# A transformer block in fp32 on one core: weight sums of the down projection paced one to a step, and SBUF tiles moved by 32 bytes

## What is computed

```python
h    = rms_norm(x, pre_mix_norm)
proj = h @ w_in
A    = forgetting_attention(fq, fk, fv, log_f)       # 8 heads x 64, causal, per-key decay
B    = gated_delta_chunked(q, k, v, g, beta)         # 4 heads x 128, chunks of 64, behind a short conv
x    = x + rms_norm(concat(A, B) @ w_out, post_mix_norm)
h    = rms_norm(x, pre_mlp_norm)
y    = square(relu(h @ w_up)) @ w_down
x    = x + rms_norm(y, post_mlp_norm)
```

## Time and profile before

| | us |
|---|---|
| median of 3 runs | 1527.16 (1526.25 to 1529.45) |
| the profiled execution, its own time | 1522.94 |
| its span | 1521.2 |
| PE busy in the span | 1408.3 (93%) |
| DVE busy | 998.5 (66%) |
| POOL busy | 679.5 (45%) |
| ACT busy | 650.0 (43%) |

### The profile page before, as it was taken

The page is one execution under the profiler, slowest core; times in us unless marked ns, Lnnn a source line. Parts: engine busy times, 40 slices in busy tenths (PEclk is TensorE's granted clock), DMA queues, the critical chain, the costliest instruction groups (busy, mean ns, idle before and its releaser), DMA issues.

```text
span 1521.2 us, 20643 instructions
## 1 busy us (share of the span) xinstructions
PE 1408.3 (93%) x7389; PEld 1179.0 (78%) x7389; DVE 998.5 (66%) x1506; ACT 650.0 (43%) x1342; POOL 679.5 (45%) x582
## 2 busy tenths in 40 slices
PE   6899999968989899898799989999999998999997
PEld 5688888857878889797688767888878776788885
DVE  6767777746566665765535697666676589744557
ACT  6554334435454553554423442233233343445453
POOL 3633333217365482753500366666567169440001
PEclk9999999989999999999799989999999999999999
DMA  6133333254132031012222224444444983333533
GB/s 202 42 119 107 108 111 111 84 181 138 29 98 70 29 98 43 15 43 65 82 90 84 76 84 152 153 153 152 153 152 139 339 309 132 95 97 95 208 97 143
DMA packets 135324, 177.87 MB, mean 117 GB/s; under 512 B 10492, under 2 KB 82732, under 8 KB 135224
## 3 DMA queue, kind: packets, MB, share of 16 engines
q1 hardware_dynamic: 135224, 176.56, 36.3%
HBM read 124.05 MB, written 52.48 MB: 116 GB/s over the span
## 4 chain that ended last, share of the span: by engine, by line
PE 60%; DVE 15%; POOL 11%; issue 5%; DMA 5%; ACT 2%; SPq 1%; POOLq 0%; DVEq 0%; ACTq 0%
PE ps L2625 6%; PE ps L2566 6%; PE ps L2568 6%; PE ps L2567 6%; PE ps L2884 5%; PE ps L2885 5%; PE ps L2886 5%; DMA w_bot<-in_w_up_dram 4%; DVE db_lo L2179 3%; DVE da_lo L2177 3%; PE ps L2750 3%; PE ps L2871 2%; PE ps L2872 2%; PE ps L2873 2%; PE ps L2825 2%
## 5 line engine op out<-in xcount | busy, mean ns | idle before, releaser
L2884 PE MATMUL ps<-db_hi,da_hi 128*128 128x512 f32 x448 | 177.6, 396 | 10.7 <-DVE db_lo L2179 10.7
L2886 PE MATMUL ps<-db_hi,da_lo 128*128 128x512 f32 x448 | 174.6, 390 | 0.0
L2885 PE MATMUL ps<-db_lo,da_hi 128*128 128x512 f32 x448 | 174.5, 389 | 0.0
L2177 DVE TENSOR_TENSOR da_lo<-a_raw,da_hi 128x512 fp32r<-128x512 f32 x112 | 103.4, 923 | 100.3 <-ACT da_hi L1663 100.3
L1663 ACT ACTIVATE da_hi<-a_raw 128x512 fp32r<-128x512 f32 x112 | 70.7, 631 | 172.4 <-PE ps L2886 150.0
L2871 PE MATMUL ps<-bt_hi,ring_hi 128*128 128x512 f32 x320 | 127.4, 398 | 3.9 <-DVE ring_lo L2099 3.6
L2873 PE MATMUL ps<-bt_hi,ring_lo 128*128 128x512 f32 x320 | 128.1, 400 | 0.0
L2872 PE MATMUL ps<-bt_lo,ring_hi 128*128 128x512 f32 x320 | 127.8, 399 | 0.0
L2436 POOL TENSOR_TENSOR o_rs<-o_ms,halves 128x1 f32<-128x1 f32 x24 | 16.5, 689 | 226.9 <-DVE o_ms L2202 111.4
L2566 PE MATMUL ps<-i_bt_hi,i_ring_hi 128*128 128x512 f32 x280 | 111.5, 398 | 3.2 <-DVE i_u L1852 3.2
L2884 PEld LDWEIGHTS ps<-db_hi,da_hi 128*128 128x128 f32 x448 | 84.0, 188 | 38.7 <-DVE db_lo L2179 21.9
(11 more groups left out here) (351 smaller groups left out, 3754.2 us busy)
## 6 DMA issues: line engine op xcount, KB each, us to landing
a_raw<-act_dram SPq DMA_DIRECT2D x112, 256.0 KB, 2.7
act_dram<-s_act SPq DMA_DIRECT2D x64, 256.0 KB, 2.0
wd<-in_w_down_dram SPq DMA_DIRECT2D x15, 1024.0 KB, 6.8
act_dram<-c SPq DMA_DIRECT2D x48, 256.0 KB, 4.9
w_top<-in_w_up_dram SPq DMA_DIRECT2D x18, 512.0 KB, 4.6
w_bot<-in_w_up_dram SPq DMA_DIRECT2D x16, 512.0 KB, 5.8
i_top<-in_w_in_dram SPq DMA_DIRECT2D x14, 512.0 KB, 4.0
i_bot<-in_w_in_dram SPq DMA_DIRECT2D x14, 512.0 KB, 5.3
```

Of the source, the lines that this page charges most:

```text
L2177: nc.vector.tensor_tensor(da_lo[s][:, :], a_raw[n % 4][:, :], da_hi[s][:, :].bitcast(F32), ALU.subtract).then_inc(d_lo_ready, 1)
L2884: nc.tensor.matmul(acc, da_hi[s][:, cols], db_hi[s][:, :], start=start, stop=False, skip_group_check=True)
L2885: nc.tensor.matmul(acc, da_hi[s][:, cols], db_lo[s][:, :], start=False, stop=False, skip_group_check=True)
L2886: return nc.tensor.matmul(acc, da_lo[s][:, cols], db_hi[s][:, :], start=False, stop=stop, skip_group_check=True)
```

## The change

Two things change. Both are in the table of addresses and in GpSimd's part of the projection down.

Addresses: every tile that started 32 bytes past a multiple of 64 now starts 32 bytes lower, on a multiple of 64 (147424 becomes 147392, 163808 becomes 163776, and so on). To make room `sums` moves from 147392 to 146944, inside a tile of constants that is used only earlier. The new addresses are 64 bytes past a multiple of 128, all of them.

```diff
-        gate_w_hi = placed("gate_w_hi", 204768, [P, KT, P], F32R)
-        gate_w_lo = placed("gate_w_lo", 208864, [P, KT, P], F32R)
+        gate_w_hi = placed("gate_w_hi", 204736, [P, KT, P], F32R)
+        gate_w_lo = placed("gate_w_lo", 208832, [P, KT, P], F32R)
...
-        I_BT_AT = {6: 147424, 7: 163808, 5: 180192, 4: 196576, 3: 212960}
+        I_BT_AT = {6: 147392, 7: 163776, 5: 180160, 4: 196544, 3: 212928}
...
-        sums = placed("sums", 147392, [P, 2, 4])
+        sums = placed("sums", 146944, [P, 2, 4])
...
-        big_hi = placed("big_hi", 163808, [P, KT, SEQ], F32R)
-        big_lo = placed("big_lo", 196576, [P, KT, SEQ], F32R)
+        big_hi = placed("big_hi", 163776, [P, KT, SEQ], F32R)
+        big_lo = placed("big_lo", 196544, [P, KT, SEQ], F32R)
...
-        BT_AT = {6: 147424, 7: 163808, 5: 180192, 4: 196576, 3: 212960}
+        BT_AT = {6: 147392, 7: 163776, 5: 180160, 4: 196544, 3: 212928}
...
-        wd = {(0, 0): placed("wd11", 45184, [P, FP, HALF]), (1, 0): placed("wd21", 147424, [P, FP, HALF]),
-              (1, 1): placed("wd22", 180192, [P, FP, HALF]), (0, 1): placed("wd12", 77952, [P, FP, HALF])}
+        wd = {(0, 0): placed("wd11", 45184, [P, FP, HALF]), (1, 0): placed("wd21", 147392, [P, FP, HALF]),
+              (1, 1): placed("wd22", 180160, [P, FP, HALF]), (0, 1): placed("wd12", 77952, [P, FP, HALF])}
```

```diff
+        PACE = {7: (8, 2), 6: (9, 2), 4: (8 + 2 * FP, 1), 5: (9 + 3 * FP, 1)}
+
         def t_count(i, kf):
-            return 3 * FP + kf + 1 if i == 5 else 3 * kf + {7: 1, 6: 2, 4: 3}[i]
+            return 2 * kf + {7: 1, 6: 2}[i] if i in (7, 6) else {4: 2, 5: 3}[i] * FP + kf + 1
...
             def t_part(i, kf):
                 b11, b12, b21, b22 = (wd[q][:, kf, :] for q in ((0, 0), (0, 1), (1, 0), (1, 1)))
+                if i in PACE:
+                    pool.wait_ge(d_lo_ready, 2 * (PACE[i][0] + PACE[i][1] * kf))
...
             for kf in range(FP):
-                for i in (7, 6, 4):
+                for i in (7, 6):
                     t_part(i, kf)
             for kf in range(FP):
+                t_part(4, kf)
+            for kf in range(FP):
                 t_part(5, kf)
```

More of the change, by code:

```diff
@@ L385, in build @@
         conv_rows = placed("conv_rows", 146880, [TAPS * 3 * GDN_HEADS, P])
-        x_in = [placed(f"x_in{s}", at, [P, D]) for s, at in enumerate((212960, 217056, 221152, 225248, 196576, 200672))]
+        x_in = [placed(f"x_in{s}", at, [P, D]) for s, at in enumerate((212928, 217024, 221120, 225216, 196544, 200640))]
         x_n = [placed(f"x_n{s}", 127232 + 4096 * s, [P, D]) for s in range(2)]
@@ L391, in build @@
         pre_row = placed("pre_row", 139520, [P, D])
-        gate_w = placed("gate_w", 163808, [P, KT, P])
-        gate_w_hi = placed("gate_w_hi", 204768, [P, KT, P], F32R)
-        gate_w_lo = placed("gate_w_lo", 208864, [P, KT, P], F32R)
+        gate_w = placed("gate_w", 163776, [P, KT, P])
+        gate_w_hi = placed("gate_w_hi", 204736, [P, KT, P], F32R)
+        gate_w_lo = placed("gate_w_lo", 208832, [P, KT, P], F32R)
         gate_y = placed("gate_y", 131328, [P, SEQ])
@@ L435, in build @@
         z_tok = [placed(f"z_tok{s}", at + 20480, [P, NT, P]) for s, at in enumerate(SET_AT)]
-        mixed_half = [placed(f"mixed_half{s}", at, [P, HT, D]) for s, at in enumerate((94336, 147424))]
+        mixed_half = [placed(f"mixed_half{s}", at, [P, HT, D]) for s, at in enumerate((94336, 147392))]
         k_split = [placed(f"k_split{s}", 110720 + 4096 * s, [P, SEQ], F32R) for s in range(2)]
@@ L459, in build @@
         wait_holder = placed("wait_holder", 146272, [P, 1])
-        c_raw = {"z": placed("c_raw_z", 163808, [P, SEQ]), "v": placed("c_raw_v", 167904, [P, SEQ]),
-                 "k": placed("c_raw_k", 180192, [P, SEQ]), "q": placed("c_raw_q", 184288, [P, SEQ])}
+        c_raw = {"z": placed("c_raw_z", 163776, [P, SEQ]), "v": placed("c_raw_v", 167872, [P, SEQ]),
+                 "k": placed("c_raw_k", 180160, [P, SEQ]), "q": placed("c_raw_q", 184256, [P, SEQ])}
         c_first = {"z": c_raw["z"], "v": c_raw["v"], "k": placed("c_first_k", 20608, [P, SEQ]), "q": placed("c_first_q", 73856, [P, SEQ])}
         v_fox_first = placed("v_fox_first", 28800, [P, SEQ])
[L465 to L478, removed]
+        v_fox = placed("v_fox", 171968, [P, SEQ])
+        decay = placed("decay", 176064, [P, NT, P])
+        kn = placed("kn", 188352, [P, 4, P])
+        qn = placed("qn", 190400, [P, 4, P])
+        knT = placed("knT", 192448, [P, 4, P])
+        qnT = placed("qnT", 194496, [P, 4, P])
+        kbg = placed("kbg", 196544, [P, 2, 4, P])
+        vb = placed("vb", 200640, [P, 2, 4, P])
+        kbT = placed("kbT", 204736, [P, 4, P])
+        n_low = placed("n_low", 208832, [P, 2, 4, P])
+        n_lev = placed("n_lev", 212928, [P, 2, 4, P])
+        t_inv = placed("t_inv", 217024, [P, 2, 4, P])
+        r_inv = placed("r_inv", 221120, [P, 2, 4, P])
+        xb = placed("xb", 225216, [P, 2, 4, P])
         gate_ps = banks(6, 2)
@@ L718, in build @@
         db_lo = [placed(f"db_lo{s}", at + 6144, [P, HALF], F32R) for s, at in enumerate(D_AT)]
-        wd = {(0, 0): placed("wd11", 45184, [P, FP, HALF]), (1, 0): placed("wd21", 147424, [P, FP, HALF]),
-              (1, 1): placed("wd22", 180192, [P, FP, HALF]), (0, 1): placed("wd12", 77952, [P, FP, HALF])}
+        wd = {(0, 0): placed("wd11", 45184, [P, FP, HALF]), (1, 0): placed("wd21", 147392, [P, FP, HALF]),
+              (1, 1): placed("wd22", 180160, [P, FP, HALF]), (0, 1): placed("wd12", 77952, [P, FP, HALF])}
         c_bot = placed("c_bot", 110720, [P, HT, D])
-        c_top = placed("c_top", 212960, [P, HT, D])
+        c_top = placed("c_top", 212928, [P, HT, D])
         sq_buf = placed("sq_buf", 135296, [P, D])
```

## The result

The changed kernel takes 1511.71 us (median of 4 runs, 1508.85 to 1514.60), the kernel before beside it 1527.66 (1526.25 to 1529.45): a ratio of 0.9901, 95% interval 0.9886 to 0.9916. It is 16 us faster; 28.5 had been forecast, and the time lies above the range of 1492 to 1510. The profiled execution took 1514.45 us with a span of 1512.7.

The account below looks back on a forecast made before the run. TensorE's matmul pace was taken to bound most projection stretches, VectorE's collisions with GpSimd the stretch from 1246 to 1310.9 us. From 1527.2 us, 12.5 (pacing) and 16.0 (addresses) were subtracted: 1498.7 us, range 1492 to 1510.

Parts of the forecast that it names:

- What bounds the kernel: TensorE's matmul time in most projection stretches; from 1246 to 1310.9 us VectorE, slowed by GpSimd, 1.09 us per collision.
- Part 1: Projection down: weight sums paced at most one per step return 19 slow steps from 3.40 to 2.72 us; 12.5 us won.
- The backlog: Projection down, steps 12 to 15: sums released late cause about seven collisions; 0.5 us of stall, between 0 and 1.5.
- Part 2: Projections in, out, up and gates: all operands on multiples of 64 bring matmuls to 0.2267 us; 16.5, less 0.5: 16.0 us.
- The addresses give nothing, as 128 counts: Rival, chance 0.10: operands still differ against 128 bytes, so the new addresses win nothing; 1514.7 us.
- TensorE's gain turns into waits: Rival, chance 0.06: stages end on another engine's work, so half of the addresses' gain is lost; 1506.7 us.
- Against: the room of VectorE and GpSimd: Argument against the rival of waits: in the projection up VectorE is busy 118.73 of 175 us, GpSimd 108.45.
- The other two rivals: Pacing gains nothing as collisions go on (0.02, 1511.2 us); an offset of 64 bytes costs more than 32 (0.02, 1529.3 us).
- the remark on the clock: Attention starts earlier and its clock's falls may shift; if a tenth of up to 25 us shifts, 2.5 us either way.

Follow-up runs that it names:

- e1: The kernel before with the paced weight sums alone, every tile at its old address: 1517.21 us, ratio 0.9926.
- e4: The changed kernel run again, unchanged: 1512.92 us, ratio 0.9913 to the kernel before.
- e3: A separate kernel without the layer: TensorE alone, 36 matmuls for each of 16 pairs of tile offsets; 0.2267 to 0.2339 us per matmul.
- e2: The kernel before with the new addresses alone, the sums in their old order: 1525.48 us, ratio 0.9980.
- e5: The changed kernel with its upper tiles another 64 bytes lower, at 128 modulo 256: 1506.17 us, ratio 0.9870 to the kernel before.
- e6: As e5, with rings 6 and 7 of the projection in also moved, 128 bytes higher: 1507.51 us, ratio 0.9875 to the kernel before.

## Why the prediction was wrong

**What bounds the kernel** was right: pace where TensorE fills the stretch, collisions from 1246 to 1311 us.

**Part 1 was right.** Forecast 12.5 us, between 11.5 and 13; e1 alone wins 12.2 at one clock and 12.8 in the projection down's own length. The steps are 2.72 us, the sums 1.29, the waits those foretold. The backlog cost 0.4 us (steps 14 and 15 took 3.00 and 2.85) where 0.5 was taken, and 0.2 to 0.8 in the profiles of e1 and e4. So a collision's 1.09 us from the rows came nearer than the Trainium skill's full exclusion (SBUF — State Buffer, Who interferes with whom), by which it would have been 2.0. The Trainium skill calls all contention of the two engines there an exclusive lock; "fully blocks" stands with VectorE's two-port modes, and an instruction with two SBUF inputs is said to contend. Not foreseen were 1.1 us at steps 6, 7 and 8 (3.04, 3.37 and 2.88 us), where `a_raw` lands late. They are no price of the change: the second profile of before has 1.0 us there too, and e1 has none.

**Part 2 was mis-sized, and this is where the prediction failed.** The step is "a matmul is slow where its two operands lie differently against 64 bytes. After the change all are on multiples of 64: all should take 0.2267". The operands' difference does count, but modulo 256, and the new differences are 64 and 192: 4.4 ns of 6.6 are won at 64, none at 192. Summed over all intervals under 245 ns, the excess over 0.2267 fell from 6.5 to 4.8 us in the projection in (5.8 forecast as won, 1.7 won), from 2.5 to 0.9 in the projection out (2.5 and 1.6), from 7.8 to 3.7 in the projection up (8.0 and 4.1), in the gates not at all. That is 7.4 instead of 16.5. One part is not explained by the differences alone: pairs at difference 0 that stand behind slow ones are slow as well, in the layer and, for up to eight matmuls, in e3. The pairs in the earlier trace rows, on which the step stood, had differences of 96, 160 and 0: they could not tell 64 bytes from 256, and the prediction said so of 128 and then gave that case 0.10. The argument against it, that the loss is 16 columns and so 64 bytes, was arithmetic, and no row.

**The rivals.** "The addresses give nothing, as 128 counts" (0.10, 1514.7) had the right doubt and nearly the right time; the truth lies between it and the forecast. The Trainium skill's rule that stood beside it (SBUF — State Buffer, Who interferes with whom: TensorE's two read ports are independent) does not give the times of this chip: alone on SBUF, the same matmul takes 0.2267 to 0.2339 us by the addresses of its two operands. "TensorE's gain turns into waits" (0.06) came true in part: of 4.1 us of pace in the projection up only 2.2 arrive in e2, and of the further 3.2 in e5 none (against e4) or 1.1 (against the first profile), until the loads come earlier. "Against: the room of VectorE and GpSimd" overlooked that an engine with room can still be late, behind a transfer. The other two rivals fell. Pacing gave its gain, and no new difference costs more than the old one in its place: 64 costs 2.2 ns where 96 cost 6.6, and 192 costs the 6.6 that 224 cost.

**The base.** The forecast was made as a difference to the median, which is sound, but the remark on the clock ("2.5 us either way") was too small for a comparison of two executions: the attention took 5.8 us more in the profile after, from the clock, and e1 took as much with the old addresses.

So: 28.5 forecast; 12.2 from part 1 and 5.5 from part 2 measured at one clock. Of part 2, 9.1 of 16.5 us were never there, as the pace was wrong. Of the 7.4 that were, 7.4 - 5.5 = 1.9 did not reach the end; in the projection up, where as much is missing, TensorE's waits for `u_buf` grew from 0.2 us to 1.2 in the changed kernel's profile; the rest was not traced. The medians, with 16.0 us, show 1.7 less than the two parts at one clock.

## What to carry to other kernels

A rule read from a few rows is worth what its rows can tell apart: list the values that they cover, ask which other rule fits them too, and see whether the change's own values are among them; here a kernel of sixteen pairs, 183 us long, would have settled it. Place the moving and the stationary tile of a long matmul stage at the same address modulo 256, not only on round addresses. When TensorE gets faster, look for loads that wait in an issue queue behind stores although their buffer is free: utilisation does not show them, the releaser of the first instruction of the chain does. And compare single executions only at the same mean granted clock, and a stage only with one that had the same clock in that stage: the projection out looked unchanged, and had won 1.5 us.

## What the runs showed that was not expected

- The pace of an fp32r matmul of 512 columns depends on moving less stationary address modulo 256: 0.2267 us at 0, 0.2289 to 0.2294 at 64, 0.2325 at 128, 0.2331 to 0.2339 at all other multiples of 32, with no other engine busy.
- Pairs at difference 0 can be slow beside others that are not: in the changed kernel a pass of 12 with `i_ba` and `i_ring_A` (both at 128) takes 2.78 us between 209.59 and 212.37, where e6 has 2.72. In e3 a pair at difference 0 was slow for its first eight matmuls behind one at 128, for three behind one at 64, and not at all behind one at 32. So the slow pace can outlast the pair that caused it; why it lasts for a whole pass of 12 in the layer is open.
- A stall of TensorE of 3.2 to 3.4 us before 70 us is in all eleven profiles of the layer. The granted clock from 66 to 84 us was then 1.00 in two of them, 0.91 in four and 0.81 in five; the two profiles of before had 0.91 and 1.00. Between e5 and e6 that alone was worth 2.5 us.
